# Two decay products in one bank pair, values centred before the scan, and dense steps dealt out by columns

## The chip, the cores and the metric

One NeuronCore of a Trainium2 chip runs the kernel; the other cores are idle. The metric is the device time of one execution in microseconds, as the median of several executions. All data are 32-bit floats. The engines are TensorE (PE in the profile's rows, PEld for its weight loads), VectorE (DVE), ScalarE (ACT), GpSimd (POOL), and SyncE (SP), which issues most of the DMA transfers.

## The reference

Two layers of a trunk run over 256 context tokens and 256 latent tokens with 1024 features. Each layer has three branches side by side, a gated convolution, an RWKV-7 scan in both directions over 16 heads of 64, and a windowed attention. It merges them and adds a feed-forward part. The second layer needs no outputs for the context. What the change touches is the scan branch:

```
w_pre = rwkv_w0 + tanh(wl) @ rwkv_w2            # both directions
decay = exp(-exp(-softplus(-w_pre) - 0.5))
a     = sigmoid(rwkv_a0 + al @ rwkv_a2)         # both directions
g     = sigmoid(gl) @ rwkv_g2
kk    = k * rwkv_k_k ; kk = kk * rsqrt(sum_head(kk*kk) + 1e-12)
...
S     = S * w + (S a) b + v k                   # scan over the tokens
y     = S r                                     # summed over both directions
mean  = mean_head(y) ; var = mean_head((y - mean)^2)
gn    = (y - mean) * rsqrt(var + GN_EPS) * rwkv_ln_g + rwkv_ln_b
out   = (gn + bonus) * g
```

## The kernel before

All activations lie transposed: 128 features on the partitions, 512 token columns (256 context, 256 latent) along the free dimension. A layer's mixing part runs over eight iterations i of 128 features each (two heads). In the first layer (`lo = 0`) all products have 512 columns. In the second (`lo = 256`) most have the latent 256, and only k and v have 512. A 32-bit product is two instructions on TensorE.

**Dense products.** Each weight strip (1024 x 128, 512 KB) comes by DMA into a ring of five buffers. A strip is eight steps, one for each 128 rows of the contraction. `dense(i)` is a generator over the six strips r, k, C, x, v, B of iteration i. It is advanced a few steps at a time by `fill(steps, n)` between the products of the scan, so that TensorE has work while ScalarE and VectorE empty a bank. During iteration i the dense steps are those of i + 1. In the last iteration they are `attention_dense()`: the keys K, the values V and the first two queries.

**PSUM.** Eight banks: two single banks that ScalarE empties (`forA`), two that the dense strips take in turn (`forG`), and two pairs of banks (`forP`) that VectorE empties. `take(F, key)` waits until the next buffer of a kind has been emptied. Every engine's program is written out in a fixed order.

**One iteration on TensorE:** `diagonal_blocks`, `head_mean(i-1)`, `turn_hats`, `turn_values`, `pair_products(0, ..)`, then eight dense steps (strip r), an `ada` group of four more strips where `MIX_ADA` names one (all eight iterations of the first layer, iterations 0 to 3 of the second), `head_var(i-1)`, `half_step`, `pair_products(1, 0)`, three steps, `corners`, `pair_products(1, 1)`, three steps, `below_left`, `value_products`, two steps, `corner_below`, `bonus_sums`, `key_sums(i+1)`, `decays(i+1)`, `through_inverse(i)`. Then comes the state loop over eight chunks of 64 tokens, with two steps after each `state_in` and each `state_out`, the rest of the steps, and `outputs(i)`. `half_step` waits for the inverse that VectorE computes from the diagonal blocks (`turn_blocks`, `join`, `spread_blocks`; its last transpose is L1909).

**The key path.** `key_sums(i+1)` needs strip k, ScalarE's `centre`, VectorE's `taps` (L1722, L1724) and `key_squares` (L1731, L1733). ScalarE turns its result into 1/norm (`key_norm`: L1310 Ln, L1312 Exp). Then come the tanh of the four decay products (L1318), the copy of the gate product (L1323), the copies of `through_inverse` (L1384) and, in `powers`, L1331 to L1334. `conv_gate` (L1392) empties strip C's bank.

**The head norm.** ScalarE copies y into `ysum` (L1401), TensorE multiplies it by `heads` (`head_mean`), VectorE makes `dev` and its square (`deviations`, L1832 and L1834), TensorE sums the squares (`head_var`), ScalarE takes the inverse root (L1351, L1354) and VectorE finishes (`normed`).

The weight ring is filled by SP in the order in which TensorE uses it (L1052 to L1054). Nearly every product goes through the helper `mm`, so nearly all matmul rows carry its line, L427.

## Time and profile before

| | |
|---|---|
| median of 3 runs | 3248.28 us (3246.55 to 3258.99) |
| the profiled execution | 3244.93 us, its span 3243.1 us |
| TensorE busy | 3009.8 us, 93% of the span |
| VectorE, ScalarE busy | 1282.1 us, 750.1 us |
| mean granted TensorE clock | 0.954 |
| first output product of iterations 0 and 7, first layer | 223.1 us, 898.6 us |
| the same, second layer | 2137.4 us, 2716.1 us |

A row of the timeline gives start, length (both in us), engine, line, operation, output and inputs, form and count. In brackets it gives how long the engine sat idle before the row and what ended that. The end of a matmul is modelled and overlaps the next row a little. The granted clock is relative: 1 is 2.4 GHz, 0.5 is 1.2 GHz.

### The profile page before, as it was taken

How to read it: one execution, taken by the hardware profiler on the slowest of the kernel's cores; microseconds unless marked ns; L12 is line 12 of the kernel's file. 1: busy time of each engine (PE TensorE's matmuls, PEld its weight loads, DVE VectorE, ACT ScalarE, POOL GpSimd, SP SyncE). 2: the span in 40 equal slices, each digit the busy share in tenths (PEclk: the TensorE clock that was granted, in tenths of full speed). 3: DMA queues.
4: the chain of work that ended last, by engine and by line, in shares of the span. 5: the costliest groups of instructions: out<-in, count | busy, mean ns of one | idle time of the engine just before them, and what ended most of it. 6: DMA issues, size and time to landing. Idle time of an engine off the chain costs nothing.

```text
span 3243.1 us, 57308 instructions
## 1 busy us (share of the span) xinstructions
PE 3009.8 (93%) x25265; PEld 1804.1 (56%) x25265; DVE 1282.1 (40%) x2596; ACT 750.1 (23%) x1440; POOL 51.8 (2%) x77
## 2 busy tenths in 40 slices
PE   7899989998988898999999999889988899999999
PEld 3455555554644444444444444566655557778887
DVE  2554555554322222012444211555555553332551
ACT  2233332233221212101111001333333332221110
POOL 1000000000000000000000000000000000000000
PEclk9899999999999999999999999888898899999999
DMA  6212222212232323322222223222211113434553
GB/s 223 75 34 62 62 56 62 69 34 62 62 98 72 101 75 91 84 76 64 77 78 78 73 71 98 69 69 69 69 43 43 43 42 99 110 112 135 149 148 119
DMA packets 499846, 264.19 MB, mean 81 GB/s; under 512 B 42848, under 2 KB 493744, under 8 KB 499088
## 3 DMA queue, kind: packets, MB, share of 16 engines
q1 hardware_dynamic: 497872, 251.50, 27.4%
q0 software_dynamic: 1728, 9.03, 0.8%
q8 instruction: 201, 3.29, 0.4%
q14 instruction: 45, 0.37, 0.0%
HBM read 255.25 MB, written 5.24 MB: 80 GB/s over the span
## 4 chain that ended last, share of the span: by engine, by line
PE 83%; DVE 8%; ACT 6%; issue 2%; DMA 1%; SPq 0%; DVEq 0%; ACTq 0%
PE psum L427 80%; ACT arena L1384 1%; DMA strips<-in_w_in_dram 1%; ACT arena L1424 1%; PE psum L784 1%; PE psum L777 1%; PE psum L853 1%; DVE arena L1881 1%; ACT L1312 1%; ACT arena L1318 1%; DVE arena L1984 0%; PE psum L614 0%; DVE arena L1724 0%; DVE arena L1722 0%; DVE arena L1855 0%
## 5 line engine op out<-in xcount | busy, mean ns | idle before, releaser
L427 PE MATMUL psum<-hT,strips 128*128 128x512 f32 (+1 forms) x4128 | 1541.9, 525 | 24.7 <-ACT hT L1251 16.4
L427 PEld LDWEIGHTS psum<-hT,strips 128*128 128x128 f32 x4128 | 781.2, 196 | 594.8 <-issue 530.3
L427 PEld LDWEIGHTS psum<-arena 32*32 32x32 f32 (+4 forms) x14592 | 384.1, 126 | 307.1 <-issue 223.8
L427 PE MATMUL psum<-arena 32*32 32x32 f32 (+6 forms) x14592 | 491.2, 226 | 63.5 <-issue 30.5
L427 PE MATMUL psum<-arena,strips 128*128 128x512 f32 (+1 forms) x1216 | 399.0, 486 | 3.0 <-DVE done L2057 3.0
L427 PEld LDWEIGHTS psum<-arena,strips 128*128 128x128 f32 x1216 | 231.1, 190 | 164.0 <-issue 144.1
L2018 DVE SCALAR_TENSOR_TENSOR arena<-arena,psum 128x512 f32<-128x512 f32 (+1 forms) x32 | 17.7, 554 | 294.0 <-PE psum L427 294.0
L1545 ACT COPY arena<-psum 128x512 f32<-128x512 f32 (+1 forms) x88 | 42.2, 479 | 390.1 <-PE psum L427 390.1
L1662 DVE TENSOR_SCALAR arena<-arena 128x512 f32<-128x512 f32 (+1 forms) x88 | 37.0, 421 | 240.1 <-ACT arena L1545 240.0
L427 PE MATMUL psum<-arena,tables 128*128 128x512 f32 (+2 forms) x232 | 87.0, 585 | 38.3 <-DVE arena L1733 32.5
L427 PE MATMUL psum<-low_rank,low_rank_out 64*128 64x512 f32 (+2 forms) x160 | 88.6, 927 | 30.5 <-ACT arena L1318 30.5
L1824 DVE TENSOR_TENSOR arena<-psum,tables 128x1024 f32<-128x1024 f32 x48 | 58.5, 1219 | 115.5 <-PE psum L427 115.5
L2168 DVE SCALAR_TENSOR_TENSOR arena<-psum,mod,arena 128x256 f32<-128x256 f32 x24 | 10.9, 481 | 208.7 <-PE psum L427 208.7
L1424 ACT ACTIVATE arena<-psum,arena 128x512 f32<-128x512 f32 (+1 forms) x96 | 58.1, 613 | 149.0 <-DVE arena L1993 148.5
L1241 ACT ACTIVATE arena<-psum,tables 128x512 f32<-128x512 f32 (+1 forms) x5 | 3.0, 601 | 369.5 <-PE psum L427 369.5
L427 PE MATMUL psum<-conv_branch,strips 128*128 128x512 f32 (+1 forms) x256 | 86.4, 490 | 1.9 <-ACT arena L1451 1.6
L1936 DVE TENSOR_TENSOR arena<-psum,arena 64x256 f32<-64x256 f32 x112 | 47.2, 421 | 100.2 <-PE psum L427 99.9
L1451 ACT ACTIVATE arena<-psum 128x512 f32<-128x512 f32 (+1 forms) x48 | 23.7, 495 | 267.8 <-PE psum L427 267.8
L427 PE MATMUL psum<-rwkv_branch,strips 128*128 128x512 f32 (+1 forms) x256 | 85.2, 486 | 0.0
L427 PE MATMUL psum<-tables,arena 128*64 128x128 f32 (+1 forms) x704 | 62.1, 276 | 23.5 <-ACT arena L1436 12.8
L427 PEld LDWEIGHTS psum<-low_rank,low_rank_out 64*128 64x128 f32 (+1 forms) x160 | 27.5, 262 | 89.5 <-ACT arena L1318 73.3
L1305 ACT ACTIVATE arena<-psum,params 128x512 f32<-128x512 f32 (+1 forms) x48 | 31.3, 652 | 198.3 <-PE psum L427 198.3
(197 smaller groups left out, 2464.4 us busy)
## 6 DMA issues: line engine op xcount, KB each, us to landing
strips<-in_w_in_dram SPq DMA_DIRECT2D x158, 512.0 KB, 4.2
strips<-in_ffn_up_dram SPq DMA_DIRECT2D x88, 512.0 KB, 3.8
strips<-in_ada_w_dram SPq DMA_DIRECT2D x80, 512.0 KB, 3.7
strips<-in_ffn_down_dram SPq DMA_DIRECT2D x32, 512.0 KB, 4.0
arena<-in_ada_w_dram SPq DMA_DIRECT2D x4, 2048.0 KB, 14.8
strips<-in_w_in_dram SPq DMA_DIRECT2D x32, 256.0 KB, 3.8
strips<-in_a_out_w_dram SPq DMA_DIRECT2D x16, 512.0 KB, 4.8
strips<-in_rwkv_out_w_dram SPq DMA_DIRECT2D x16, 512.0 KB, 5.2
```

Source lines behind the costliest of these rows:

```text
L427: return pe.matmul(o, lhs, rhs, start=start, stop=stop)
L777: pe.matmul(o[rows(h), t], GG[rows(h), c, d, :], AR[i % 2][d][rows(h), c, 1, back], start=fresh[h], stop=False, skip_group_check=True)
L784: ins = pe.matmul(o[rows(h), t], RV[:, c, d, h, :], EE[:, 1, c // 4, d, h, c % 4, back], start=False, stop=True, skip_group_check=True)
L853: ins = pe.transpose(PS[:, BANK_A[s.b], k * P:(k + 1) * P], pr[n % 2][:, h * T + k * P:h * T + (k + 1) * P], tab["ident"])
L1312: act.activation(rinv_k, rinv_k, ACT.Exp, scale=-0.5).then_inc(ev["rinv_ready"], 1)
L1318: act.activation(v[:, :, ::-1] if j % 2 else v, o, ACT.Tanh, bias=pp[:, 19 + j, i:i + 1], scale=0.5).then_inc(s.free, 1)
L1384: ins = act.copy(EE[r, k0:3, m // 2, :, :, 2 * (m % 2) + p].rearrange("p k d h t -> p k (d h) t").rearrange("p k q t -> p q k t"), PS[r, B ...
L1424: ins = act.activation(pr[u][:, x:x + 2 * T // g], PS[:, b0 + x // T, x % T:x % T + 2 * T // g], ACT.Exp, bias=st[:, u, 1, i:i + 1], accum ...
L1545: act.copy(upp[:, b, lo // SEG:, 1:SEG + 1], s.o[:, lo:T].rearrange("p (s t) -> p s t", t=SEG)).then_inc(s.free, 1)
L1662: ts(dst, src[:, :, 1:n + 1], g1, None, MUL).then_inc(s_vec, 1)
L1824: tt(EE[:, 0:2, j, d].rearrange("p k h c t -> p k (h c) t").rearrange("p k q t -> p q k t"), o, mask.unsqueeze(1).broadcast_to([P, 8, 2, C ...
L1936: tt(dst, o, add, ADD).then_inc(s.free, 1)
```

## The change

- The four decay products of an iteration go in two takes of a bank pair (`forP`) instead of four takes of a single bank. The two products of a take use the two halves of the rows and one bank each. ScalarE still computes four tanh, and VectorE waits for the first pair before its first scaling.
- The values are turned with a matrix that also subtracts the mean of each head (`centre`) instead of the identity, so y comes out of the scan centred. `head_mean`, `deviations` and the buffer `ysum` go. ScalarE's `outputs` squares y into `rinv_g` and copies it into `dev`.
- A generator step yields its number of 256-column units, and `fill` takes units. The shares between the products are new and differ by layer. In the first layer they are, in steps, 8, 5, 3, 2 and 2, the last ones after `bonus_sums`, and two in each place of the state loop; none is left for the tail. In the second layer they are 8 units, 6 more behind the `ada` group and ahead of `head_var`, then 6, 4, 3 and 3, and 2.4 in each place of the state loop. Strip C thereby begins ahead of `key_sums(i+1)`.
- Ahead of iteration 0 of a layer strip C is done before `key_sums(0)`.
- ScalarE's `conv_gate(i+1)` moves between the two `powers`. VectorE's `keys` in the last iteration move. `one` is `pe.matmul` with start and stop set, so each product now carries its own line.

```diff
-                for k in range(KT):
+                b, free = rg.last[0], rg.free
                     ins = mm(s.o[:, first:T], strip[:, b, k, :], rhs[:, k, first:T], k == 0, k == KT - 1)
-                    if k == 0:
+                    if k < KT - 1:
                         pay(ins)
...
-                    yield
+                    yield (T - first) // SEG
...
                 def decays(i):
                     pe.wait_ge(*lr.full())
-                    for j in range(4):
-                        q, r = j // 2, rows(j % 2)
-                        s = take(A, f"decay{j}", l, i)
-                        mm(PS[:, BANK_A[s.b], :], lw[r, q, :], low[r, q, :]).then_inc(s.full[0], 1)
+                    for q in range(2):
+                        s = take(Q, f"decay{q}", l, i)
+                        for h in range(2):
+                            ins = one(PS[:, BANK_P[s.b] + h, :], lw[rows(h), q, :], low[rows(h), q, :])
+                        ins.then_inc(s.full[0], 1)
...
-                                ins = mm(PS[rows(1 - p), BANK_A[s.b], m * P:(m + 1) * P], v, tab["ident"])
+                                ins = one(PS[rows(1 - p), BANK_A[s.b], m * P:(m + 1) * P], v, tab["centre"])
...
-                def head_mean(i):
-                    pe.wait_ge(*slots["y", l, i].freed)
-                    s = take(Q, "mean", l, i)
-                    mm(PS[:, BANK_P[s.b], lo:T], tab["heads"], ysum[:, lo:T]).then_inc(s.full[0], 1)
...
+                over = [0]
+                def fill(steps, columns):
+                    over[0] += columns
+                    while over[0] > 0:
+                        n = next(steps, 0)
+                        if n == 0:
+                            over[0] = 0
+                        over[0] -= n
...
-                fill(steps, 2 * KT)
+                fill(steps, 32 if wide else 24)
+                fill(steps, 16 if wide else 8)
                 key_sums(0)
                 pe.wait_ge(ev["low_ready"], l + 1)
                 decays(0)
                 pe.drain().then_inc(lr.free, 1)
-                fill(steps, 4 * KT)
+                fill(steps, everything)
...
                     diagonal_blocks(i)
-                    if i > 0:
-                        head_mean(i - 1)
...
-                    fill(steps, KT)
+                    fill(steps, 16 if wide or not ahead else 8)
                     if MIX_ADA[l][i]:
                         ada_group(*MIX_ADA[l][i])
+                    if lo and ahead:
+                        fill(steps, 6)
...
                     pair_products(1, 0, i)
-                    fill(steps, 3)
+                    fill(steps, 10 if wide else 6)
                     corners(i)
                     pair_products(1, 1, i)
-                    fill(steps, 3)
+                    fill(steps, 6 if wide else 4)
                     below_left(i)
                     value_products(i)
-                    fill(steps, 2)
+                    fill(steps, 4 if wide else 3)
                     corner_below(i)
                     bonus_sums(i)
+                    fill(steps, 4 if wide else 3)
...
                         if c > 0:
-                            fill(steps, 2)
+                            fill(steps, 4 if wide else 2.4)
                         if c < NCH - 1:
                             state_out(c, i)
-                            fill(steps, 2)
-                    fill(steps, 5 * KT)
+                            fill(steps, 4 if wide else 2.4)
+                    fill(steps, everything)
                     outputs(i)
...
                 def outputs(i):
                     s = filled("y", i)
-                    act.copy(ysum[:, lo:T], PS[:, BANK_A[s.b], lo:T]).then_inc(s.free, 1)
+                    if i > 0:
+                        act.wait_ge(ev["tail_done"], at(i - 1))
+                    act.activation(rinv_g[:, lo:T], PS[:, BANK_A[s.b], lo:T], ACT.Square).then_inc(ev["devsq_ready"], 1)
+                    act.copy(dev[:, lo:T], PS[:, BANK_A[s.b], lo:T]).then_inc(s.free, 1)
...
                         powers(0, i + 1)
+                        conv_gate(i + 1)
                         powers(1, i + 1)
-                        conv_gate(i + 1)
...
-                def deviations(i):
-                    s = filled("mean", i)
-                    stt(dev[:, lo:T], PS[:, BANK_P[s.b], lo:T], -1.0 / HD, ysum[:, lo:T], MUL, ADD).then_inc(s.free, 1)
-                    dve.wait_ge(*s.freed)
-                    tt(rinv_g[:, lo:T], dev[:, lo:T], dev[:, lo:T], MUL).then_inc(ev["devsq_ready"], 1)
...
-                        if not ahead and c in (4, 6):
-                            keys(c // 2 - 2)
+                        if not ahead and c == (6 if lo else 3):
+                            keys(0)
+                        if not ahead and c == 5 and lo == 0:
+                            keys(1)
...
+                if lo:
+                    keys(1)
                 query(0)
```

## Rows read from the trace of the kernel before

**Rows 1.** The page: busy times, and the chain that ended last by engine.
```profile
PE 3009.8 (93%) x25265; PEld 1804.1 (56%) x25265; DVE 1282.1 (40%) x2596; ACT 750.1 (23%) x1440; POOL 51.8 (2%) x77
...
PE 83%; DVE 8%; ACT 6%; issue 2%; DMA 1%; SPq 0%; DVEq 0%; ACTq 0%
```

**Rows 2.** Tile psum, TensorE alone: what ended its idle time, us and times.
```profile
  DVE arena L1733: 32.5, 16
  ACT arena L1318: 30.5, 31
```

**Rows 3.** Windows: seven iterations, first and second layer; busy times, clock, DMA.
```profile
core 0: us, PE busy (x) PEld busy (x) DVE busy (x) ACT busy (x) POOL busy (x), PEclk, DMA share, GB/s
223.10:898.60 675.50, 623.52 (x8732) 367.36 (x8731) 349.52 (x628) 208.84 (x336) 13.77 (x15) 0.97 0.21 58
2137.40:2642.00 504.60, 448.67 (x6853) 301.66 (x6852) 281.19 (x559) 171.54 (x294) 11.37 (x12) 0.89 0.20 54
```

**Rows 4.** Timeline of TensorE, iteration 4 of the first layer.
```profile
518.86 1.13 PE L427 MATMUL psum<-arena,tables 128*128 128x512 f32 x2
...
562.52 1.10 PE L427 MATMUL psum<-arena,tables 128*128 128x512 f32 x2 [1.57 <-DVE arena L1733]
563.54 1.13 PE L427 MATMUL psum<-low_rank,low_rank_out 64*128 64x512 f32 x4
566.91 1.70 PE L427 MATMUL psum<-low_rank,low_rank_out 64*128 64x512 f32 x4 [2.24 <-ACT arena L1318]
...
572.23 2.67 PE L427 MATMUL psum<-arena 64*64 64x128 f32 x40 [0.40 <-ACT arena L1384]
574.82 1.99 PE L427 MATMUL psum<-hT,strips 128*128 128x512 f32 x4
```

**Rows 5.** Timeline of ScalarE, the same iteration.
```profile
520.46 1.08 ACT L1339 COPY arena<-psum 128x512 f32<-128x512 f32 x2 [2.23 <-PE psum L614]
...
563.65 0.69 ACT L1310 ACTIVATE arena<-psum,tables 128x512 f32<-128x512 f32 x1 [1.25 <-PE psum L427]
...
566.19 1.25 ACT L1318 ACTIVATE arena<-psum,params 128x512 f32<-128x512 f32 x2
568.07 1.26 ACT L1318 ACTIVATE arena<-psum,params 128x512 f32<-128x512 f32 x2 [0.64 <-PE psum L427]
569.97 0.59 ACT L1323 COPY arena<-psum 128x512 f32<-128x512 f32 x1 [0.64 <-PE psum L427]
571.00 4.75 ACT L1384 COPY arena<-psum 64x512 f32<-64x512 f32 x8 [0.45 <-PE psum L427]
575.78 0.63 ACT L1331 ACTIVATE arena<-arena 128x512 f32<-128x512 f32 x1
...
577.09 0.61 ACT L1331 ACTIVATE arena<-arena 128x512 f32<-128x512 f32 x1
```

**Rows 6.** Timeline of TensorE, second layer, iterations 1, 1, 2 and 5.
```profile
2185.27 2.05 PE L427 MATMUL psum<-arena,tables 128*128 128x512 f32 x2 [2.00 <-DVE arena L1733]
...
2199.55 1.13 PE L427 MATMUL psum<-hT,strips 128*128 128x256 f32 x4
...
2244.72 1.31 PE L427 MATMUL psum<-arena 32*32 32x32 f32 x128 [2.13 <-DVE arena L1909]
...
2494.39 3.51 PE L427 MATMUL psum<-arena 32*32 32x32 f32 x144 [4.04 <-DVE arena L1909]
```

**Rows 7.** Timeline of VectorE, second layer.
```profile
2182.34 0.75 DVE L1722 SCALAR_TENSOR_TENSOR arena<-psum,params,arena 128x510 f32<-128x510 f32 x1 [3.89 <-ACT arena L1305]
...
2184.43 0.69 DVE L1733 TENSOR_TENSOR arena<-arena 128x512 f32<-128x512 f32 x1
...
2483.60 0.41 DVE L1832 SCALAR_TENSOR_TENSOR arena<-psum,arena 128x256 f32<-128x256 f32 x1
```

**Rows 8.** DMA: an issue by SP, second layer; size and time to landing by line.
```profile
2240.50 0.37 SPq L1054 DMA_DIRECT2D strips<-in_w_in_dram  x1
...
strips<-in_w_in_dram SPq DMA_DIRECT2D x158, 512.0 KB, 4.2
```

**Rows 9.** Timeline of TensorE, start of the first layer's attention.
```profile
908.45 2.07 PE L427 MATMUL psum<-arena,tables 128*128 128x512 f32 x2 [3.12 <-DVE arena L1834]
```

More of the change, by code:

```diff
@@ L1 @@
 from contextlib import ExitStack
+from functools import partial
 import numpy as np
@@ L280, in trunk @@
         low = sb("low_rank", 3, T)
[L281 removed]
+        ARENA = 30896
         arena = sb("arena", ARENA)
@@ L424, in _ @@
             F_BANK = {"psum_act": BANK_A, "psum_dense": BANK_G, "psum_pair": BANK_P}
-            def mm(o, lhs, rhs, start=True, stop=True):
-                return pe.matmul(o, lhs, rhs, start=start, stop=stop)
+            mm, one = pe.matmul, partial(pe.matmul, start=True, stop=True)
             def quad(q):
@@ L932, in merged_out @@
                     square_sum(2 * l + 1, KT - 1, lo)
-                def fill(steps, n):
-                    for _ in range(n):
-                        next(steps, None)
+                over = [0]
[6 more added lines that the diff above has]
+                        over[0] -= n
+                wide = lo == 0
+                everything = 1000
                 steps = dense(0)
-                fill(steps, 2 * KT)
+                fill(steps, 32 if wide else 24)
+                fill(steps, 16 if wide else 8)
                 key_sums(0)
@@ L1314, in decays @@
                 def decays(i):
[L1315 to L1319 removed]
+                    for q in range(2):
+                        s = filled(f"decay{q}", i)
+                        for d in range(2):
+                            o, v = seg2(PS[:, BANK_P[s.b] + d, :]), seg2(th[:, 2 * q + d, :])
+                            ins = act.activation(v[:, :, ::-1] if d else v, o, ACT.Tanh,
+                                                 bias=pp[:, 19 + 2 * q + d, i:i + 1], scale=0.5)
+                        ins.then_inc(s.free, 1)
                     s = filled("g", i)
```

72 lines of the change are left out of this document (29 added, 43 removed).

## The prediction

> **What bounds the kernel now.** I read the page first. TensorE is busy for 93% of the span and holds 83% of the chain that ended last [rows 1]. So a change pays here only by taking TensorE work away, by filling a wait of TensorE, or by keeping its clock up. The next view is TensorE's own releasers, in the answer for the tile psum [rows 2]: 32.5 us were waited for VectorE's key squares (L1733, once per iteration, 16 times), and 30.5 us for ScalarE's decay tanh (L1318). Both sit in the mixing part, which the change rewrites, and so does a wait for the last transpose of the inverse (L1909), which shows in the second layer alone [rows 6]. The windows of seven iterations in each layer [rows 3] show 52 us (675.5 - 623.5) and 56 us (504.6 - 448.7) without a matmul, and a mean granted clock of 0.97 and 0.89. At full clock the mean would be 1 and at the lower of the two levels 0.5, so some 40 us (6% of 675) and some 110 us (22% of 505) ran at 1.2 GHz. Then I followed one iteration of each layer, engine by engine.
>
> "First layer" below is the one with 512 columns everywhere, "second layer" the one where most products have 256. K is the moment when the key sums (one product) end.
>
> **Term A, the head mean goes.** One product of 128x512, 1.13 us with its modelled tail [rows 4], call it 1.0; eight times, and eight times half of that: 12 us. Its second operand came from ScalarE's copy and its result went through two VectorE instructions (`deviations`), 0.41 us and as much again in the second layer [rows 7]. Those leave VectorE's chain to the inverse. ScalarE now squares y and copies it, where it copied alone. After that copy (0.59 us, as the gate's) it sat idle for 2.23 us until the turned hats, at 520.46 [rows 5]; with the mean gone that is 0.59 + 2.23 - 1.0 = 1.8 us of room, and two instructions of 0.6 to 0.7 us fit. I cost it at nothing. Without that cover (a table load ahead of the square that isn't done while ScalarE waits for y) the turned hats would come late by up to 1 us, at most 14 us in all. Centring the values costs nothing: the same products with another constant operand.
>
> **Term B, key squares.** TensorE waits 1.57 us per iteration before the key sums in the first layer [rows 4] and 2.00 us in the second [rows 6]. The key strip used to end two matmul groups before them. Now it ends before `below_left`, and four more dense steps (first layer) or six narrow ones (second) lie between. ScalarE takes the key strip only after its `value_products` copies, earlier than now, and VectorE needs 2.8 us after it (2182.34 to the end of L1733 at 2185.1, [rows 7]); two steps of 0.9 us (four instructions in 1.99 us with the tail, [rows 4]) on top of the work already there reach past that. The wait goes: 7 x 1.57 + 7 x 2.00 = 25 us. The dense steps for this come from the tail ahead of `outputs`, where the trace shows no wait; two steps (about 1.7 us) stay there, against one short VectorE sum.
>
> **Term C, decays.** Now each of the four decay products takes one bank of ScalarE's pair. The first two run together, four instructions in 1.13 us, and then TensorE waits 2.24 us for a tanh, and 0.40 us in the inverse [rows 4]. It is tempting to book all of that. But TensorE has no dense steps between the key sums and the first state step, and ScalarE's own chain is nearly closed: Ln from 563.65, tanh from 566.19, 568.07, the gate copy 569.97, the eight inverse copies from 571.00 for 4.75 us [rows 5]. With all products there early that chain is 2.54 (Ln and exp) + 1.25 + 1.26 + 0.59 = 5.64 us from 563.65, so the inverse copies begin at 569.3 and not at 571.0. The gain is what ScalarE waited, 1.6 to 1.7 us, not 2.84. First layer: 7 x 1.6 = 11 us. The decay banks now belong to VectorE's pair; the one before them (`bonus`) is emptied right after the key squares, so nobody waits there.
>
> **Term D, a new wait for the conv gate.** Dense strips alternate between two banks. C used to stand behind the key sums in that order and now stands ahead, so strip x takes the bank that C filled, and `conv_gate` on ScalarE must empty it first; before, strip x took the bank of the key sums, long free. First layer: C ends with the second fill of the state loop, ScalarE's copy takes 0.59 us, with some 0.1 us at each end, and only one state group lies between, which I take as 0.4 us: 0.4 us lost, 7 times, 3 us. Second layer: C ends in the first fill, and strip x starts in it. ScalarE then still has inverse copies, `powers(0)` (575.78 to 577.09, 1.3 us, [rows 5]) and the gate. From K: 2.54 + 2.51 + 0.37 for the chain, then the copies, paced by the two banks, to about K + 9.7, powers to 11.0, gate to 11.4. TensorE would be there at about K + 9.9, so it stands 1.6 us, and queued behind it are state_in(1) and, through that, VectorE. Before, the first fill came at K + 12.25 (2199.55 - 2187.3, [rows 6]), after at K + 8.9: a gain of 3.4 less 1.6, 1.8 us at full clock, near 0 if the stage runs at the lower clock as it does now. I take 1.0, seven times: 7 us. That strip x waits less if `powers(0)` comes later than the gate is ruled out: ScalarE's order puts it first.
>
> **Term E, the wait for the inverse in the second layer.** In iterations 4 to 6 TensorE waits about 4.0 us (4.04 ahead of 2494.39, [rows 6]). Three k steps of 0.9 us now stand ahead, and VectorE is 0.8 us earlier without `deviations`: about 3.0 us gained, three times, 9 us. In iterations 0 to 3 the same three steps stand behind the `ada` group, which eats four strips in 2 us out of a ring of five. The k strip is issued at 2240.50 and, with the median of 4.2 us, lands at 2244.7 [rows 8]: exactly when the 2.13 us wait now ends (2244.72). So there a DMA wait takes the place of the VectorE wait and the steps come on top, in place of later ones: 0 to -1 us each, -2 us in all. Sum 7 us.
>
> **Term F, the rest.** Attention begins with a wait of 3.12 us for `deviations(7)` [rows 9]; its input is now ready with y. With a third of that in the second layer: 4 us. In iteration 7 of the second layer ScalarE's `keys(1)` stands ahead of `corner_below`, and the K strip ends later: -1 us. At the start of each layer strip C covers the key wait, but strip x then stands for `conv_gate(0)`, behind both `powers`, from about K + 3 to K + 10; against the old order this nets +1 us each, 2 us.
>
> **The clock.** A product that takes 1.10 us in the first layer takes 2.05 us in the second, right after the 2.00 us wait [rows 4, 6]. Where waits go, the clock should fall less often. I take 3.5 us for the key sums (half of 7 x 1.0) and 8 us for iterations 4 to 6 and the attention start, of an upper bound of half of the 150 us at the lower level, 75 us. The lower bound is a loss: the waits of term D may lower the clock over dense steps.
>
> Sum: A 12 + B 25 + C 11 - D 3 + 7 + E 7 + F 5 + clock 11.5 = 75.5 us. The profiled execution took 3244.9 us, 3.4 us under the median of 3248.3. So 3248.3 - 75.5 = 3173, and with the tie towards what I left unpriced (the wait for the y copy before attention, the second layer's short stops in the state loop, which I put at some 3 us) **3170 us**.
>
> **Rivals.** Changes under 0.5% (16 us) can't be told from none here.
>
> *The waits only move.* The filled waits come back as the new ones: D, the DMA wait of E, and ScalarE's chain. For it: ScalarE really is nearly closed through that stage. Against: terms A and B don't rest on it. It leaves A, half of B, attention: 12 + 12 + 4 = 28 us, 3220 us. Chance 0.13.
>
> *The clock stays up.* If most of the time at the lower level goes, some 45 us come on top: 3125 us. For it: the low stretches sit at these waits. Against: the small products around them stay. Chance 0.08.
>
> *The clock falls over dense work (slower).* The wait for the conv gate stands just ahead of the state loop's dense steps. If it lowers the clock and the loop's short stops keep it there, each us costs half a us. To turn 75 us into a loss it needs over 11 us at the lower level in each of 14 iterations; at 15 us each the loss is 105 us and the time 3248 - 75 + 105 = 3278 us. For it: the second layer already has such stretches. Against: the loop is dense, 4 of 5 us in it are full products. Chance 0.05. The Trainium skill speaks for this rival ("TensorE: Matmul & The Clock Gate", "A second HAM failure mode: psum-queue depth-cycling"): short idle times between matmul groups that cycle through PSUM banks make the clock swing and cost throughput. The trace agrees that it swings, 0.89 on the mean; it doesn't show at this place what one wait does.
>
> *Nothing moves.* The waits sit beside stalls that TensorE has anyway ("issue"), which grow by what is saved: 3248 us. Chance 0.06.
>
> *Forecast as worked out*, 3140 to 3200 us: 0.68.
>
> The range: 3130 to 3215 holds the forecast and part of the neighbours, some 0.8. Faster by over 0.5%: 0.68 + 0.13 (28 us is over 16) + 0.08 = 0.89, less 0.02 for the near edge of the second case: 0.87. Same 0.08, slower 0.05.
>
> **What the profile after would show.** No product by the head mean (A). No wait before the key sums (B); if one stands there, VectorE is the late one. Between K and the first fill about 9.6 us in the first layer, not 11.2 (C); if it is still 11, ScalarE wasn't waiting for products. A wait for the conv gate ahead of strip x, 0.4 us and 1.6 us (D); if it is over 4 us, the forecast is too low. A wait for a strip's DMA behind the `ada` groups of the second layer, and none over 1.5 us at the inverse in iterations 4 to 6 (E). Mean clock in the second layer's mixing 0.91 or more. What would make me wrong: a clock of 0.85 or less there, or "issue" idle well over the present tens of us.

## The result and the profile after

The changed kernel takes 3131.75 us (median of 4 runs, 3127.84 to 3133.05), the kernel before 3247.99 us (3246.55 to 3258.99): a ratio of 0.9634 [0.9617, 0.9652]. That is 116 us by the medians and 119 by the ratio; I call it 118 below. The sign was right and the size wrong: I forecast 3170 us and a range from 3130 to 3215, and 3248.3 x 0.9634 is 3129. The rival "the clock stays up" (3125 us), to which I gave 0.08, came nearest.

The page of the changed kernel, busy times and chain by engine (answers to [rows 1]). The profiled execution took 3132.01 us, its span 3130.2 us, mean granted clock 0.973:

```profile
PE 2926.4 (93%) x25233; PEld 1763.4 (56%) x25233; DVE 1267.4 (40%) x2564; ACT 749.0 (24%) x1456; POOL 51.5 (2%) x77
...
PE 87%; ACT 6%; DVE 3%; issue 2%; DMA 2%; SPq 0%; DVEq 0%; ACTq 0%
```

Only 32 matmul instructions are gone, but TensorE is busy for 83 us less, of which those 32 are some 12. Products that are still there got shorter, and that is the clock. TensorE's idle time (span less busy) fell by 29.5 us, from 233.3 to 203.8.

Windows of the same iterations (answers to [rows 3]): iterations 1 to 7 of the first layer, 1 to 6 of the second, and the last of the second, for which the row of before is added below.

```profile
core 0: us, PE busy (x) PEld busy (x) DVE busy (x) ACT busy (x) POOL busy (x), PEclk, DMA share, GB/s
215.90:846.20 630.30, 599.84 (x8717) 356.32 (x8716) 342.60 (x617) 209.53 (x343) 14.38 (x16) 0.99 0.23 62
2068.90:2525.90 457.00, 410.36 (x6843) 281.42 (x6842) 277.56 (x547) 170.26 (x300) 11.38 (x12) 0.96 0.22 60
2525.90:2606.30 80.40, 74.40 (x1199) 56.80 (x1198) 32.06 (x70) 19.52 (x35) 2.92 (x4) 0.94 0.18 43
```
```profile
2642.00:2716.10 74.10, 70.35 (x1199) 54.06 (x1198) 31.01 (x70) 19.25 (x34) 2.92 (x4) 1.00 0.19 46
```

([Rows 3] and the prediction call their second window seven iterations; it is six.) The first layer gained 45.2 us, the second 47.6 us, and the last iteration of the second lost 6.3 us. The start to the first outputs went from 223.1 to 215.9 us, and from attention to the second layer's first outputs 1238.8 us became 1222.7 us. With 3 us behind it all that is the 113 us between the spans. Time without a matmul fell from 52.0 to 30.5 us in the first window and from 55.9 to 46.6 us in the second. Time at 1.2 GHz, by the mean clocks, fell from some 40 to some 13 us and from some 110 to some 37 us.

TensorE's releasers (answers to [rows 2]):

```profile
  ACT arena L1400: 27.6, 16
  issue: 27.3, 23
  ACT arena L1331: 25.5, 14
  DMA strips<-in_w_in_dram: 20.1, 10
```

The key squares and the tanh have left the list. The conv gate (L1400), the gate copy ahead of the inverse (L1331) and the strips' DMA have entered it. The first and the last stand in the prediction by name (D and E); the second is ScalarE's chain, which term C takes for the bound.

**Where the time went.** I cut each iteration at K (end of the key sums) and at the first dense step of the state loop. Windows of that stretch in the kernel before: four of the seven of the first layer, their sum and mean, and one of the second layer:

```profile
175.14:187.91 12.77, 10.92 (x83) 6.15 (x82) 5.10 (x7) 9.32 (x15) 0.00 (x0) 0.78 0.01 1
269.90:283.87 13.97, 11.03 (x84) 6.32 (x83) 5.10 (x7) 9.32 (x15) 0.00 (x0) 0.76 0.00 0
...
563.54:574.82 11.28, 8.34 (x83) 4.92 (x82) 5.10 (x7) 9.31 (x15) 0.00 (x0) 1.00 0.01 2
658.64:672.66 14.02, 11.23 (x84) 6.48 (x83) 5.11 (x7) 9.35 (x15) 0.00 (x0) 0.76 0.00 0
...
sum 90.76, PE 71.42 PEld 41.28 DVE 35.72 ACT 65.24 POOL 0.00; mean PE 10.20 PEld 5.90 DVE 5.10 ACT 9.32 POOL 0.00
...
2187.24:2199.55 12.31, 10.82 (x83) 6.53 (x82) 5.10 (x7) 7.97 (x14) 0.00 (x0) 0.56 0.01 1
```

The same in the changed kernel, first layer (every one of the seven is 9.34), then two of the second layer:

```profile
174.51:183.85 9.34, 7.61 (x84) 4.70 (x83) 4.92 (x7) 8.97 (x15) 0.00 (x0) 1.00 0.01 2
...
sum 65.38, PE 53.26 PEld 32.88 DVE 34.44 ACT 62.82 POOL 0.00; mean PE 7.61 PEld 4.70 DVE 4.92 ACT 8.97 POOL 0.00
...
2033.21:2043.13 9.92, 7.79 (x83) 5.62 (x83) 5.11 (x7) 7.94 (x15) 0.00 (x0) 0.83 0.01 2
...
2199.25:2207.88 8.63, 6.22 (x84) 4.08 (x83) 4.25 (x6) 7.99 (x15) 0.00 (x0) 1.00 0.01 2
```

In the first layer the stretch took 13.0 us on the mean before, at clocks from 0.76 to 1, and takes 9.34 us at full clock now. In the second the seven together took 84.8 us, at clocks from 0.55 to 0.72, and take 65.2 us. [Rows 4], on which term C rests, show iteration 4, the only one of the seven that ran at full clock. The usual one is below: TensorE in iteration 1 of the kernel before.

```profile
269.90 1.13 PE L427 MATMUL psum<-low_rank,low_rank_out 64*128 64x512 f32 x4
273.27 2.65 PE L427 MATMUL psum<-low_rank,low_rank_out 64*128 64x512 f32 x4 [2.23 <-ACT arena L1318]
276.12 2.07 PE L427 MATMUL psum<-low_rank,low_rank_out 128*128 128x512 f32 x2 [0.20 <-ACT arena L1318]
278.12 2.75 PE L427 MATMUL psum<-arena 64*64 64x128 f32 x32
```

The wait for the tanh is the same 2.2 us, but the products behind it are slower: the gate's 128x512 product takes 2.07 us here and 1.12 us in the changed kernel, whose iteration 4 follows:

```profile
537.58 1.99 PE L590 MATMUL psum<-low_rank,low_rank_out 64*128 64x512 f32 x8
539.50 1.12 PE L593 MATMUL psum<-low_rank,low_rank_out 128*128 128x512 f32 x2
540.55 1.09 PE L724 MATMUL psum<-arena 64*64 64x128 f32 x16
543.15 2.14 PE L724 MATMUL psum<-arena 64*64 64x128 f32 x32 [1.51 <-ACT arena L1331]
...
551.87 1.98 PE L451 MATMUL psum<-hT,strips 128*128 128x512 f32 x4 [0.29 <-ACT arena L1400]
```

Nothing stands between the decay products any more. TensorE now runs 3.0 us of products and 1.1 us of the inverse before it stops, and in the first layer the products behind that stop are at full rate. In the second that stop is 2.13 us long, and in four iterations of seven the products behind it ran slow (3.99 us for 48 instructions, 2.62 at full rate). Those four stretches took 9.7 to 9.9 us at a clock of 0.82 to 0.83, the other three 8.63 us.

### The profile page after: what moved, and what is told of

It reads as the page before. It is cut to its first block, busy times and chain, and to the rows that moved or that the text cites. A ratio compares the mean times of both kernels' runs of the same rounds, so it can differ in the third digit from the quotient of the medians.

```text
span 3130.2 us, 57225 instructions
## 1 busy us (share of the span) xinstructions
PE 2926.4 (93%) x25233; PEld 1763.4 (56%) x25233; DVE 1267.4 (40%) x2564; ACT 749.0 (24%) x1456; POOL 51.5 (2%) x77
## 4 chain that ended last, share of the span: by engine, by line
PE 87%; ACT 6%; DVE 3%; issue 2%; DMA 2%; SPq 0%; DVEq 0%; ACTq 0%
PE psum L451 56%; PE psum L1018 7%; PE psum L472 2%; PE psum L638 2%; DMA strips<-in_w_in_dram 1%; PE psum L724 1%; PE psum L741 1%; ACT arena L1325 1%; PE psum L755 1%; PE psum L706 1%; PE psum L791 1%; PE psum L839 1%; PE psum L486 1%; PE psum L861 1%; PE psum L518 1%
## 5 line engine op out<-in xcount | busy, mean ns | idle before, releaser
L451 PEld LDWEIGHTS psum<-hT,strips 128*128 128x128 f32 x3968 | 742.7, 194 | 576.9 <-issue 485.8
L724 PE MATMUL psum<-arena 64*64 64x128 f32 (+1 forms) x1024 | 67.8, 283 | 29.8 <-ACT arena L1331 25.5
L724 PEld LDWEIGHTS psum<-arena 64*64 64x64 f32 x1024 | 56.5, 146 | 45.3 <-ACT arena L1331 28.1
L638 PE MATMUL psum<-arena 64*128 64x128 f32 (+1 forms) x1024 | 75.3, 290 | 6.9 <-issue 6.9
L741 PEld LDWEIGHTS psum<-arena 64*64 64x64 f32 x896 | 35.0, 134 | 67.3 <-issue 49.0
```

The lines of the kernel that those rows point to most:

```text
L451: ins = mm(s.o[:, first:T], strip[:, b, k, :], rhs[:, k, first:T], k == 0, k == KT - 1)
L638: ins = one(PS[:, b0 + h, (c % 4) * n:(c % 4 + 1) * n], BK[d][rows(h), c].rearrange("p j t -> p (j t)"), ar[d][rows(h), c, 0:n // CH].rear ...
L724: ins = one(PS[r, BANK_A[s.b], q * n:(q + 1) * n].rearrange("p (k t) -> p k t", t=CH), TLR[r, 8 * h + 4 * d + m].rearrange("p b t -> p (b ...
L741: ins = one(PS[r, BANK_P[s.b] + h, d * CH:(d + 1) * CH], AR[i % 2][d][rows(h), c, 0, :], GG[rows(h), c, d, :])
```

## The experiments

My theory after the result: the stop for the tanh lowers the clock for the stretch behind it. The rivals: the stop for the key squares does it; the dense steps ahead of the key sums do it (the shares); the run varies by itself. "Stretch" below is K to the first dense step, the seven of the first layer.

| kernel | median us | ratio to before, 95% | clock of the profile |
|---|---|---|---|
| shares_alone | 3201.96 | 0.9869 [0.9841, 0.9897] | 0.965 |
| old_shares | 3179.45 | 0.9798 [0.9774, 0.9822] | 0.963 |
| centre_alone | 3239.5 | 0.9983 [0.9969, 0.9998] | 0.949 |
| decays_alone | 3190.01 | 0.9820 [0.9797, 0.9842] | 0.966 |
| busy_wait | 3238.98 | 0.9980 [0.9966, 0.9994] | 0.960 |
| steps_in_decays | 3203.42 | 0.9859 [0.9837, 0.9880] | 0.966 |
| gate_late | 3146.31 | 0.9687 [0.9667, 0.9708] | 0.972 |
| keys_after | 3128.2 | 0.9627 [0.9606, 0.9648] | 0.976 |
| steps_in_inverse | 3117.35 | 0.9601 [0.9581, 0.9622] | 0.977 |
| k_after_var | 3142.16 | 0.9683 [0.9665, 0.9700] | 0.969 |
| all_three | 3121.43 | 0.9617 [0.9591, 0.9643] | 0.972 |
| changed_again (the changed kernel) | 3134.81 | 0.9653 [0.9629, 0.9676] | 0.971 |
| inverse_second | 3102.88 | 0.9557 [0.9544, 0.9571] | 0.977 |
| inverse_one_step | 3113.27 | 0.9568 [0.9546, 0.9591] | 0.976 |

### The change without its parts

**shares_alone** is the kernel before with the units, the new shares and the moved `conv_gate` and `keys`; head mean and decays stay.

```diff
-                    fill(steps, 2)
+                    fill(steps, 4 if wide else 3)
                     corner_below(i)
                     bonus_sums(i)
+                    fill(steps, 4 if wide else 3)
                     if ahead:
                         key_sums(i + 1)
```

> The kernel before with the dense shares of the change alone (units, new fills, the place of conv_gate and of keys); four decay takes, head mean and deviations as before. Theory (most of what came beyond the forecast is TensorE's clock, kept up because the shares fill its stops): key waits gone (25 us), one wait for the conv gate added (about 10 us), a few us at the inverse, and some 30 to 45 us by the clock: 3170 to 3195 us, mean clock 0.965 or more. Rival (the shares only move waits, the gain is in the work taken away): 3215 to 3240 us, clock as before, 0.954.

It gained 44 us, less than expected. The waits for the key squares are gone, so that part holds. The stop for the tanh stayed, and with it the slow stretch of the first layer. The sum row of its windows there, and six iterations of the second layer:

```profile
sum 91.65, PE 71.77 PEld 42.14 DVE 35.72 ACT 65.42 POOL 0.00; mean PE 10.25 PEld 6.02 DVE 5.10 ACT 9.35 POOL 0.00
...
2117.60:2596.50 478.90, 425.59 (x6853) 290.83 (x6852) 281.67 (x558) 171.07 (x294) 11.41 (x12) 0.94 0.21 57
```

91.65 us against 90.76 before: for the first layer the theory that the shares carry the clock falls. For the second it holds. Six iterations took 478.9 us for 504.6, at a clock of 0.94 for 0.89, and 23 of these 26 us are TensorE's busy time for the same instructions (448.7 to 425.6). The seven stretches took 80.5 us for 84.8.

**old_shares** is the other half: the changed kernel with the shares of before.

```diff
-                    fill(steps, 4 if wide else 3)
+                    fill(steps, 2)
                     corner_below(i)
                     bonus_sums(i)
-                    fill(steps, 4 if wide else 3)
```

> The changed kernel with the dense shares of the kernel before (steps, not units; conv_gate and keys in their old places): centred values and decay pairs only. Theory: head mean 12 us, attention start 4 to 7 us, ScalarE's closed chain 11 to 20 us, hardly any clock: 3205 to 3225 us, mean clock 0.955 to 0.960, the key waits of 1.57 and 2.00 us still there. Rival (the work taken away carries the gain): 3170 us or less.

It gained 66 us, more than the theory had and less than its rival. TensorE still waited 1.57 us (first layer) and 2.00 us (second) for the key squares, yet every stretch of the first layer took 9.34 us. So the key wait isn't what makes the stretch of the first layer long.

**centre_alone** centres the values and drops the head mean on the kernel before.

```diff
-                                ins = mm(PS[rows(1 - p), BANK_A[s.b], m * P:(m + 1) * P], v, tab["ident"])
+                                ins = mm(PS[rows(1 - p), BANK_A[s.b], m * P:(m + 1) * P], v, tab["centre"])
...
-                    if i > 0:
-                        head_mean(i - 1)
```

> The kernel before with the centred values alone: no head mean product, no deviations, ScalarE squares and copies y. Theory: 8 x 1.0 + 8 x 0.55 us of products, 3 + 1 us of waits at the attention start, 0.3 us per iteration at the inverse of the second layer: 3228 to 3235 us, clock unchanged within 0.003. If ScalarE's square costs TensorE time, the turned hats come late and the gain is under 8 us. Rival (centring feeds the clock): 3210 us or less.

It gained some 6 us of the 12 that term A gives. Its profile has a clock of 0.949 (0.954 before), so part of the twelve was lost again there, in the first layer: the seven iterations took 682.5 us for 675.5, at a clock of 0.94 for 0.97. What lowered it, its rows don't settle.

**decays_alone** puts the decay products in two takes of the bank pair on the kernel before.

```diff
-                    for j in range(4):
-                        q, r = j // 2, rows(j % 2)
-                        s = take(A, f"decay{j}", l, i)
-                        mm(PS[:, BANK_A[s.b], :], lw[r, q, :], low[r, q, :]).then_inc(s.full[0], 1)
+                    for q in range(2):
+                        s = take(Q, f"decay{q}", l, i)
+                        for h in range(2):
+                            ins = mm(PS[:, BANK_P[s.b] + h, :], lw[rows(h), q, :], low[rows(h), q, :])
+                        ins.then_inc(s.full[0], 1)
```

> The kernel before with the decay pairs alone. In the changed kernel the stretch from the end of the key sums to the first dense step of the state loop takes 9.34 us in every first-layer iteration; before it took 11.3 us in the one iteration that the forecast read and 12.8 to 14.0 us in the others, which ran it partly at the lower clock. Theory (the pairs close ScalarE's chain, so the stretch no longer depends on the clock): 9.3 us in the first layer and 8.6 us in the second, in all iterations, and 3248 - 7 x 3.6 - 7 x 3.4 - 2 x 3.5 = 3192 us or a few us less. Rival (old_shares gained by the clock that centring gives the next stage): stretch shorter by 1.6 us only, 3220 us or more.

It gained 58 us, as the theory had it, and that is half of the whole change, where term C and the second layer's gain (the conv gate's wait taken off) gave 18. Three of its windows, two first-layer ones at different clocks and one of the second:

```profile
168.71:178.05 9.34, 7.61 (x84) 4.70 (x83) 4.92 (x7) 8.98 (x15) 0.00 (x0) 1.00 0.01 2
...
551.85:561.18 9.33, 8.72 (x83) 5.18 (x82) 4.91 (x7) 8.97 (x15) 0.00 (x0) 0.88 0.01 3
...
2069.47:2078.10 8.63, 7.88 (x83) 4.45 (x82) 4.25 (x6) 7.98 (x15) 0.00 (x0) 0.80 0.01 2
```

The stretch takes 9.34 and 8.63 us whatever the clock, with ScalarE busy for 8.97 of the 9.34: its chain closes the stretch now, as term C says. Before, ScalarE had still waited some 1.7 us for products in iteration 4, the one at full clock, and in the other six TensorE at the low clock made the stretch longer still. No work was taken away here, 25265 matmul instructions as before, and TensorE was busy for 43 us less. Not all of the stretch's gain stayed, though: the seven of the first layer gained 25 us, and the seven iterations around them 12 (663.5 us for 675.5, at a clock of 0.96 for 0.97), so some of the low clock came back outside the stretch. The three parts add up roughly: 58 + 44 + 6 = 108 of 118 us.

### Which stop lowers the clock

**busy_wait** computes products that nobody uses while TensorE waits for the key squares of the kernel before, 24 products in all.

```diff
                     s = take(G, "kk", l, i)
+                    for _ in range(2 if lo else 1):
+                        mm(s.o, ones[:, :], hT[:, 0, :])
                     pe.wait_ge(ev["kk_sq_ready"], at(i))
```

> The kernel before with more work: in the wait ahead of the key sums TensorE computes a product into the same bank (ones by one step's columns of hT, 512 columns) once in the first layer and twice in the second, which the key sums then overwrite. 24 products more (24 us at full clock), all inside the waits of 1.57 and 2.00 us. Theory (these stops pull the clock down): the waits shrink below 0.7 us, the key sums and decays of the second layer run at full clock, mean clock 0.957 or more, time 3225 to 3240 us although work was added. Rival (the clock follows something else, such as the small products around): 3246 to 3256 us, clock 0.954.

More work made it about 6.5 us faster, with an interval that just excludes 1, and the clock rose from 0.954 to 0.960, as the theory had it. Two of its stretches in the second layer:

```profile
2185.88:2195.61 9.73, 6.95 (x83) 4.29 (x83) 4.57 (x7) 7.99 (x14) 0.00 (x0) 1.00 0.01 2
...
2516.04:2528.12 12.08, 9.84 (x83) 6.16 (x82) 5.11 (x7) 8.09 (x14) 0.00 (x0) 0.72 0.00 0
```

The seven of the second layer took 79.9 us for 84.8, at clocks from 0.71 to 1.00 for 0.55 to 0.72, and those of the first 88.6 us for 90.8, though TensorE still stops 2.24 us for the tanh in all of them. So the stop for the key squares lowers the clock too, mostly in the second layer. All in all that is a fraction of what the changed kernel gained.

**steps_in_decays** leaves the waits for the tanh where they are and does dense steps in them, two wide or four narrow ones.

```diff
-                def decays(i):
+                def decays(i, steps=None):
...
                         mm(PS[:, BANK_A[s.b], :], lw[r, q, :], low[r, q, :]).then_inc(s.full[0], 1)
+                        if j == 1 and steps is not None:
+                            fill(steps, 4 if lo else 2)
```

> The kernel before with 1.8 us of dense work (two steps of strip C in the first layer, four narrow ones in the second) between the second and the third decay product, where TensorE waits 1.3 to 2.2 us for a tanh; the decays stay in four takes. Theory (that stop is what keeps the clock low in the stretch): the added work costs nothing there, the clock of the stretch rises, and it takes 11.3 to 11.6 us in the first layer in spite of the steps; 14 x 1.8 us of steps taken from elsewhere plus about 15 us by the clock: 3205 to 3215 us, low-clock time in the stretch under half of before (98 us in 14 iterations). Rival (the small products of the stretch pull the clock down, stop or no stop): low-clock time as before, 3222 to 3235 us.

It gained 45 us: TensorE was idle for 17 us less and busy for 31 us less, with the same instructions. The first of its windows and the sum of the first layer:

```profile
176.26:187.54 11.28, 10.26 (x87) 5.60 (x86) 5.10 (x7) 9.31 (x15) 0.00 (x0) 1.00 0.17 48
...
sum 79.70, PE 72.46 PEld 39.34 DVE 35.72 ACT 65.19 POOL 0.00; mean PE 10.35 PEld 5.62 DVE 5.10 ACT 9.31 POOL 0.00
```

The stretch now holds some 1.8 us of dense work more and is shorter: five of the seven took 11.28 us, the time of the one at full clock before. With the stop filled the clock stays up, with the key wait in place. The dense work that was added might do that by itself, but decays_alone adds none and also keeps the clock of the stretch at 0.88 or more there. Together they show it for the first layer: the stop for the tanh lowers the clock. In the second layer both stops have a part, since the clock of the stretch rose when either was filled (steps_in_decays: 75.4 us for 84.8, clocks from 0.82 to 0.93). Why iteration 4 of the kernel before kept its clock through the same stop stays open, and what the clock does outside the stretch was not taken apart by cause.

### The costs that the change brought

**gate_late** puts `conv_gate` behind both `powers` again in the changed kernel.

```diff
                         powers(0, i + 1)
-                        conv_gate(i + 1)
                         powers(1, i + 1)
+                        conv_gate(i + 1)
```

> The changed kernel with conv_gate back behind both powers on ScalarE, which lengthens the one wait that the change adds. It is 0.29 us (first layer) and 1.6 us (second) long now. Theory (the wait costs TensorE its length and no more): about 1.3 us longer in each of 7 iterations of the second layer, under 0.5 us in the first, since powers(1) fits ahead of the end of strip C: 3140 to 3146 us. Rival (each such stop also lowers the clock over the state loop behind it): 3155 us or more, with low-clock time in the state loops.

14.6 us slower than the changed kernel, or 11.5 than changed_again below. The wait of the second layer grew from 1.6 to 2.88 us in most iterations, which is 9 us for seven. The rest of the state loop behind that wait, iteration 1, in the changed kernel and then in gate_late:

```profile
2131.44:2152.90 21.46, 21.46 (x152) 12.02 (x152) 14.19 (x34) 2.41 (x5) 0.00 (x0) 1.00 0.26 74
```
```profile
2135.16:2159.10 23.94, 23.94 (x152) 13.49 (x153) 14.21 (x34) 1.19 (x2) 0.00 (x0) 0.89 0.23 66
```

In gate_late six of the seven loops of the second layer took 23 to 24 us, at clocks of 0.89 to 0.93, for 21.5 us at full clock. In four profiles of kernels with the 1.6 us wait (the changed kernel, changed_again, keys_after, k_after_var) 6 of 28 loops ran below full clock. So the longer wait costs its length and some clock over the dense work behind it. The slower rival's mechanism is real, but small: 3 to 5 us at 1.2 GHz in such a loop, where the rival needed over 11 in each iteration.

**keys_after** moves ScalarE's copy of the last keys behind `corner_below` in the second layer's last iteration, which had lost 6.3 us.

```diff
                     if ahead:
                         centre(1, "k", i + 1, 0)
-                    else:
+                    elif lo == 0:
                         keys(1)
                     corner_below(i)
+                    if not ahead and lo:
+                        keys(1)
```

> The changed kernel with ScalarE's keys(1) behind corner_below in the last iteration of the second layer alone. That iteration went from 74.1 us (before) to 80.4 us with the change, with a wait of 1.86 us for the corner copies at the inverse and 10.2 us at the lower clock where there was none. Theory (keys(1) holds up the corner copies, the stop costs the clock): the wait falls under 0.7 us, the iteration takes 73 to 76 us, 3126 to 3129 us in all. Rival (only the wait is lost, the clock falls for another reason): 78 to 79 us, a gain of 1 to 2 us.

Its window of that iteration, which answers to the third row of the windows after:

```profile
2520.20:2594.80 74.60, 69.92 (x1197) 54.35 (x1196) 32.01 (x71) 19.52 (x35) 2.92 (x4) 1.00 0.19 46
```

74.6 us for 80.4, and the clock back at 1.00. A wait of 1.86 us for the corner copies had drawn some 10 us of low clock behind it. The whole kernel moved by 3.6 us, and the intervals of the two ratios overlap.

**steps_in_inverse** does dense steps in the wait for the gate copy (four units in the first layer, two in the second) and, in the second, empties strip C's bank after ScalarE's second inverse copy. **k_after_var** moves six units behind `pair_products(1, 0)` in the iterations where an `ada` group empties the ring. **all_three** has both and keys_after. **changed_again** is the changed kernel beside them.

```diff
                         ins.then_inc(s.full[0], 1)
+                        if ahead and m == 0:
+                            fill(steps, 4 if wide else 2)
...
                         ins.then_inc(s.free, 1)
+                        if lo and i < KT - 1 and m == 1:
+                            conv_gate(i + 1)
...
                         powers(0, i + 1)
-                        conv_gate(i + 1)
+                        if lo == 0:
+                            conv_gate(i + 1)
```
```diff
-                    if lo and ahead:
+                    late = 6 if lo and ahead and MIX_ADA[l][i] else 0
+                    if lo and ahead and not late:
                         fill(steps, 6)
...
-                    fill(steps, 10 if wide else 6)
+                    fill(steps, 10 if wide else 6 + late)
```

> The changed kernel with dense steps inside through_inverse, behind its first group, where TensorE waits 1.51 us (first layer) or 2.13 us (second) for the gate copy: two steps of strip C in the first layer, the last two narrow ones in the second; there conv_gate moves ahead of ScalarE's third inverse copy. Theory (these waits are free room and ScalarE has 1 us of idle time between its inverse copies): 1.3 us per iteration in the first layer, 0.9 us plus the 1.6 us wait for the conv gate in the second, 7 x 1.3 + 7 x 2.5 = 26 us: 3103 to 3110 us. Rival (ScalarE's chain is closed there, and what is put in holds it up): the stretch from the key sums to the state loop grows by as much, 3122 us or more.

> The changed kernel with the three k steps of iterations 0 to 3 of the second layer not behind the ada group but behind the first pair product of direction 1, where strip k has long landed. Theory: the wait of 2.7 to 3.3 us for the strip's DMA becomes the wait for the inverse that stood there before, 1.3 to 2 us: 4 to 7 us gained, 3125 to 3128 us. Rival (the stop costs the same wherever it ends): within 2 us of the changed kernel.

> The changed kernel with steps_in_inverse, k_after_var and keys_after together. Theory (three separate places): 26 + 5 + 3.5 = 34.5 us under the changed kernel, 3094 to 3102 us. Rival (the stops share one ScalarE chain): 3110 us or more.

> The changed kernel, unaltered, beside the three others on the same chip, to compare them with: 3128 to 3135 us.

The windows of steps_in_inverse for the two layers:

```profile
214.00:853.70 639.70, 603.19 (x8716) 359.94 (x8716) 344.20 (x618) 208.84 (x343) 14.36 (x16) 0.98 0.23 61
2071.00:2509.10 438.10, 402.26 (x6840) 276.20 (x6840) 276.70 (x546) 169.59 (x300) 11.38 (x12) 0.98 0.23 62
```

The kernel gained 17 us on changed_again, between the theory and its rival. The second layer gained 19 us on the 457.0 of the changed kernel (26 on the 463.9 of changed_again). The first lost 9 us: its conv gate wait grew to 0.66 us, and with no steps left for the state loop's last place TensorE waited 0.53 us for VectorE ahead of the outputs. k_after_var was 7 us slower than changed_again by the medians, against what was expected, but the intervals of the two ratios overlap. Iterations 1 to 3, which it touches, took 79.4, 78.1 and 79.0 us, and 83.8, 79.3 and 77.1 us in changed_again. Its profiled execution was already 3.7 us behind at the second layer's first decay products, ahead of everything that it alters. So no loss is shown for the move itself. all_three was no better than steps_in_inverse alone, 19 us above the top of its forecast: the gains don't add up.

**inverse_second** keeps what gained: the steps in the inverse and the early `conv_gate` in the second layer alone, with keys_after. **inverse_one_step** adds one dense step in the first layer's wait (`lo or 1` where inverse_second has `lo or 0`).

```diff
+                        if ahead and m == 0 and (lo or 0):
+                            fill(steps, 2)
```

> The changed kernel with keys_after, and with the two narrow steps and the early conv_gate inside through_inverse in the second layer only. Theory (the 1.6 us wait for the conv gate and part of the 2.13 us wait go; nothing of the first layer is touched): 7 x 2.3 + 3.5 = 20 us under the changed kernel, about 3112 us, with the first layer's windows back at 628 us for seven iterations. Rival (the loss that steps_in_inverse shows in the first layer, 639.7 us, is chance of the clock): no better than steps_in_inverse's 3117 us.

> As inverse_second, with one step (0.9 us) in the first layer's wait of 1.51 us, where two were too long and left no step ahead of outputs. Theory (one fits): the stretch from the key sums to the state loop stays at 9.34 us with the step inside, 0.5 to 0.9 us gained in each of 7 iterations: 3107 to 3110 us. Rival (each step that leaves the tail is missed there, where outputs waits for VectorE's last sum): first layer's windows 630 us or more, no gain over inverse_second.

inverse_second is the best version: 3102.88 us, 0.9557 [0.9544, 0.9571] of the kernel before, 29 us under the changed one by the medians and 25 by the ratios, and 9 us under the theory. Its second layer's six iterations take 437.4 us, and its first layer's seven 628.8 us. One stretch of the second layer, and the product behind the gate copy:

```profile
2032.52:2041.15 8.63, 7.28 (x87) 4.76 (x86) 4.24 (x6) 8.25 (x16) 0.00 (x0) 1.00 0.01 2
```
```profile
2265.49 2.62 PE L724 MATMUL psum<-arena 64*64 64x64 f32 x48 [1.08 <-ACT arena L1333]
```

ScalarE's chain sets the length as before (8.63), with dense steps inside now, and the wait is 1.08 us where the changed kernel has 2.13. All seven stretches of the second layer now take 8.63 us at full clock, where four had been longer. The conv gate's wait is gone. The step in the first layer brought nothing (its seven iterations took 633.6 us for 628.8). TensorE was idle there for 2 us less, but busy for 7 us more with the same instructions, so in that profile the clock took back what the step saved.

## Why the prediction was right and wrong

**Waits (right by name).** Each wait that I named came or went. None stands ahead of the key sums (B). The conv gate's is 0.29 us in the first layer, for 0.4, and some 1.6 us in the second, for 1.6 (D). Both kinds of row, timeline of TensorE in the second layer of the changed kernel:

```profile
2087.98 4.61 PE L451 MATMUL psum<-hT,strips 128*128 128x512 f32 x5 [3.31 <-DMA strips<-in_w_in_dram]
...
2280.64 3.99 PE L724 MATMUL psum<-arena 64*64 64x64 f32 x48 [2.13 <-ACT arena L1331]
...
2287.70 0.70 PE L451 MATMUL psum<-hT,strips 128*128 128x256 f32 x2 [1.44 <-ACT arena L1400]
```

The wait for strip k's DMA behind the `ada` groups is there in iterations 0 to 3, 2.7 to 3.3 us (E), and the wait for the inverse in iterations 4 to 6 is 1.3 to 1.5 us, for about 1. At the start of the second layer TensorE waits 7.32 us for `conv_gate(0)`, where I had K + 3 to K + 10. Attention begins without a stop (F). Their sum was smaller than mine: TensorE's idle time fell by 29.5 us, where terms B to F come to 52. Part of that is the clock again, since slow products eat into the wait behind them: in the kernel before the wait for the tanh is 1.29 us where the decay products ahead of it ran slow, and 2.24 us where they didn't.

**Term A came out smaller.** 12 us forecast; alone it brought some 6, with a lower clock, so what it is worth at an equal clock isn't shown.

**Term C, the step that failed by size.** The mechanism is right: ScalarE's chain is nearly closed and closes the stretch at 9.34 us, 1.94 us under the 11.28 of iteration 4, for 1.6. But I took the stretch of before from one iteration, and it was the only one of seven at full clock. The seven took 90.76 us and now take 65.38: 25 us, for 11. In the second layer the stretches shrank from 84.8 to 65.2 us, 20 us, where I had booked 7 for them and the conv gate together, on the ground that the gain would be near 0 at the low clock. It was the reverse: at the low clock TensorE, not ScalarE, sets the stretch, so a full clock is worth more there. Most of this miss is the clock's, so it must not be added to the next one.

**The clock term, the step that failed in kind.** I priced the clock at 11.5 us of an upper bound of 75, and put it at the key sums and the inverse, because there the trace had a slow product right behind a wait. The stop for the tanh got no clock price at all. The runs showed it to be the dearer one: decays_alone, which removes it, made TensorE's busy time 43 us shorter for the same instructions. In the first layer shares_alone shows that the key waits go and the stretch stays slow, and steps_in_decays and decays_alone show that the tanh stop governs. In the second layer the places that I had priced do count, and for more than 11.5 us: shares_alone, which clears the key wait and shortens the one for the inverse, took 23 us off TensorE's busy time there. The rest of my sum, 64 us, with half of the 100 us less at 1.2 GHz that the windows show, makes 114 us, close to the 118 measured. That is the rival "the clock stays up". That it comes so close is luck in part, since the waits gave 29.5 us and not 52. TensorE's busy time fell by 83 us, where term A and the clock term come to 23.5. My reason against the rival, that the small products around the stops stay, was wrong: in the first layer they run at full clock once the stop among them is gone, and in inverse_second in both.

**The slower rival.** Its mechanism is there, and a small one, as gate_late shows. I gave it 0.05.

**Small misses.** Iteration 7 of the second layer lost 6.3 us, for 1: I saw that ScalarE's `keys(1)` stood ahead of `corner_below`, and not the low clock behind the wait. "Issue" waits fell to 27.3 us, so "nothing moves" has no support.

## What to carry to other kernels

A stop's price is its length and the clock of what comes behind it. Before a stretch is priced from one iteration, list it for all of them with the granted clock beside: where the same code takes 11.28 and 14.02 us, the difference is what a filled stop can give back. And ask at each clock which engine closes the stretch, since a gain that is small at full clock may be double at half. Where two kernels run the same matmul instructions, the difference of TensorE's busy times is, roughly, the clock's share of the gain, and the rest is the waits'.

Where a stop sits among small products, either fill it with dense steps (steps_in_decays, 45 us) or give the products banks so that none waits (decays_alone, 58 us). The second keeps the steps for another place. A fixed number of dense steps pays where the longest wait is: two units moved into the second layer's inverse paid, one step there in the first layer did not.

## What the hardware showed unexpectedly

24 useless products in a wait made the kernel 6.5 us faster. A stop of 2.2 us for the tanh left the stretch behind it up to 2.7 us longer than at full clock (14.02 for 11.28), but not each time. The places of the low clock also differ between executions of one kernel: six iterations of the second layer took 457.0 us in one profile of the changed kernel and 463.9 us in another. Dense work isn't safe either: behind a wait of 2.88 us the state loop, where TensorE never stopped, took up to 23.9 us for 21.5.
